# First attention's query and key projections: one 512-column matmul with the weights' high half in place of two of 256, in three banks

## The reference, cut to what matters

```python
hn = rmsnorm(h, norm_mix[l])
proj = jnp.einsum('bsd,de->bse', hn, w_in[l])
(fq, fk, fv, ff, gq, gk, gv, ga, gb, gz, gate_fox, gate_gdn) = split_in(proj)
y_fox = fox_attention(fq.reshape(...), fk.reshape(...), fv.reshape(...), log_f)
# logit[t,s] = q_t.k_s / sqrt(128) + decay, causal, softmax, times v
...
o = gated_delta_rule(q, k, v, g, beta)   # chunks of 64, a triangular solve in each
...
h = h + jnp.einsum('bse,ed->bsd', y, w_out[l])      # then a feed-forward part
```

## Time and profile before

| | |
|---|---|
| median of 3 runs | 806.86 us (806.81 to 808.23) |
| the profiled execution | 807.0 us, its span 805.6 us |
| PE busy | 798.9 us (99% of the span), granted clock 1.0 |
| DVE busy | 592.9 us (74%) |
| ACT busy | 448.9 us (56%) |
| steps 41 to 56 | from 143.34 us to about 204 us of the span |

### The profile page before, as it was taken

How to read it: one execution, slowest core, us unless ns; L and a number is a source line. 1 busy time by engine, 2 the same in 40 slices (tenths; PEclk the granted TensorE clock), 3 DMA queues, 4 the chain that set the end, 5 groups by cost and what they waited for, 6 DMA issues and landing times.

```text
span 805.6 us, 13987 instructions
## 1 busy us (share of the span) xinstructions
PE 798.9 (99%) x5608; PEld 721.3 (90%) x5608; DVE 592.9 (74%) x1001; ACT 448.9 (56%) x729; POOL 74.4 (9%) x65
## 2 busy tenths in 40 slices
PE   8999999999999999999999999999999999999998
PEld 6999998999999989899999998887878888888887
DVE  6888878875454776769999996486766777778543
ACT  6666577554535554556656564366665655655441
POOL 0001000010011203001101110021100111011000
PEclk9999999999999999999999999999999999999999
DMA  7855564547432554575687655555425656656542
GB/s 261 241 163 162 178 228 145 172 121 223 126 114 86 175 170 158 200 241 179 196 253 242 221 191 203 171 194 166 148 81 169 204 176 207 190 177 208 184 162 73
DMA packets 126257, 144.15 MB, mean 179 GB/s; under 512 B 11488, under 2 KB 103024, under 8 KB 125936
## 3 DMA queue, kind: packets, MB, share of 16 engines
q1 hardware_dynamic: 123744, 141.22, 55.1%
q10 hardware_dynamic: 2448, 2.03, 1.0%
HBM read 141.78 MB, written 1.46 MB: 178 GB/s over the span
## 4 chain that ended last, share of the span: by engine, by line
PE 97%; DMA 1%; DVE 1%; ACT 1%; SPq 0%; issue 0%; DVEq 0%; ACTq 0%
PE bank L579 94%; DMA panel_raw<-in_w_in 1%; PE bank L633 1%; PE bank L943 0%; DVE panel_lo L1557 0%; PE bank L665 0%; PE bank L892 0%; ACT panel_hi L1080 0%; PE bank L916 0%; PE bank L720 0%; ACT x_halves L1080 0%; PE bank L822 0%; SPq L2358 0%; DVE h L1986 0%; DVE h L1998 0%
## 5 line engine op out<-in xcount | busy, mean ns | idle before, releaser
L1557 DVE TENSOR_TENSOR panel_lo<-panel_raw,panel_hi 128x1024 fp32r<-128x1024 f32 x251 | 313.5, 1252 | 144.8 <-ACT panel_hi L1080 144.2
L579 PE MATMUL bank<-x_halves,panel_hi 128*128 128x256 f32 (+1 forms) x1952 | 416.0, 305 | 1.0 <-DVE x_halves L1993 0.7
L1080 ACT ACTIVATE panel_hi<-panel_raw 128x1024 fp32r<-128x1024 f32 (+1 forms) x253 | 266.8, 1057 | 164.2 <-PE bank L579 160.7
L579 PEld LDWEIGHTS bank<-x_halves,panel_hi 128*128 128x128 f32 x1952 | 315.8, 191 | 16.9 <-issue 0.9
L579 PE MATMUL bank<-x_halves,panel_lo 128*128 128x256 f32 x1152 | 324.8, 282 | 0.0
L579 PEld LDWEIGHTS bank<-x_halves,panel_lo 128*128 128x128 f32 x1152 | 219.8, 191 | 0.0
L579 PE MATMUL bank<-panel_hi,x_halves 128*128 128x512 f32 x256 | 80.6, 396 | 0.0
L579 PE MATMUL bank<-panel_hi,act_hi 128*128 128x512 f32 x176 | 68.6, 390 | 0.0
L579 PE MATMUL bank<-panel_hi,act_lo 128*128 128x512 f32 x176 | 68.5, 389 | 0.0
L579 PE MATMUL bank<-panel_lo,act_hi 128*128 128x512 f32 x176 | 68.5, 389 | 0.0
L579 PEld LDWEIGHTS bank<-panel_hi,x_halves 128*128 128x128 f32 x256 | 46.8, 188 | 9.9 <-DVE panel_lo L1557 0.6
(11 more groups left out here) (289 smaller groups left out, 927.6 us busy)
## 6 DMA issues: line engine op xcount, KB each, us to landing
panel_raw<-in_w_in SPq DMA_DIRECT2D x38, 1024.0 KB, 5.3
panel_raw<-in_w_up SPq DMA_DIRECT2D x30, 1024.0 KB, 5.4
panel_raw<-in_w_down SPq DMA_DIRECT2D x20, 1024.0 KB, 5.1
panel_raw<-in_w_gate SPq DMA_DIRECT2D x10, 1024.0 KB, 5.3
panel_raw<-in_w_out SPq DMA_DIRECT2D x8, 1024.0 KB, 5.0
panel_raw<-in_w_in SPq DMA_DIRECT2D x11, 512.0 KB, 4.6
panel_raw<-in_w_branch_fox SPq DMA_DIRECT2D x4, 1024.0 KB, 4.9
panel_raw<-in_w_branch_gdn SPq DMA_DIRECT2D x4, 1024.0 KB, 5.2
```

The lines of the kernel that those rows point to most:

```text
L579: return e.matmul(o, l, r, start=start, stop=stop, skip_group_check=True)
L1080: return e.activation(o, i_, ACT.Copy, scale=scale)
L1557: e.tensor_tensor(lo, raw_view(i, k0, kt), hi.bitcast(F32), ALU.subtract).then_inc(s_lo, 1)
```

## The change

The eight panels of fq and fk become `hl`. Each of their 16 groups takes a bank of its own from a new ring "fqk" of the banks 4, 0 and 1, in this order: fq 0: 4, 0; fk 0: 1, 4; fq 1: 0, 1; fk 1: 4, 0; fq 2: 1, 4; fk 2: 0, 1; fq 3: 4, 0; fk 3: 1, 4. The ring "side" gives up bank 4 from n = 41 and gets it back at n = 58. ACT's `fox_project` goes. In its place ACT copies the low sum of each group to SBUF (`fqk_low_copy`, 256 columns, two per panel), and DVE adds the high sum from PSUM and the copy (`fqk_sum`, 256 columns, two per panel), which empties the bank.

```diff
     for j in range(4):
         for kind, c0 in (("fq", C_FQ), ("fk", C_FK)):
-            add((kind, j), "mix", True, "w_in", 0, KD, c0 + j * PW)
+            out.append(((kind, j), "mix", "hl", "w_in", 0, KD, c0 + j * PW, PW))
...
+FQK = [(kind, j) for j in range(4) for kind in ("fq", "fk")]
...
+        fqk_low = [at(f"fqk_low{i}", [P, 2, T], 17.5, skip=2048 * i) for i in range(2)]
...
-        rings = {"few": [0, 1], "fox": [2, 3], "side": [4, 5, 6, 7], "gemm": [0, 1, 2, 3]}
+        rings = {"few": [0, 1], "fqk": [4, 0, 1], "fox": [2, 3], "side": [4, 5, 6, 7], "gemm": [0, 1, 2, 3]}
...
-            if key[0] == "z" or key in (("fv", 0), ("fq", 0), ("fk", 0)):
+            if key[0] == "z" or key == ("fv", 0):
                 return "fox"
+            if key in FQK:
+                return "fqk"
...
-        HALVES_OF = {"norm2": x_halves, "yf": yf_halves, "yg": yg_halves}
+        HALVES_OF = {"mix": x_halves, "norm2": x_halves, "yf": yf_halves, "yg": yg_halves}
...
-                e.wait_ge(*emptied(("fq", hh // 2)))
-                e.wait_ge(*emptied(("fk", hh // 2)))
+                e.wait_ge(*emptied(("fq", hh // 2, hh % 2)))
+                e.wait_ge(*emptied(("fk", hh // 2, hh % 2)))
...
+                if n == FIRST_HALF["fq", 0] + 1:
+                    rings["side"] = [5, 6, 7]
+                if n == END["fk", 3] + 2:
+                    rings["side"] = [4, 5, 6, 7]
                 gemm(n)
...
-            def fox_project(kind, j):
-                e.wait_ge(*product((kind, j)))
-                dst, scale = (qfT, float(DH) ** -0.5) if kind == "fq" else (kfT, 1.0)
-                copy(dst[:, 2 * j:2 * j + 2, :], pairs(bank_of((kind, j))), scale).then_inc(empties((kind, j)), 1)
+            def fqk_low_copy(kind, j):
+                p = FQK.index((kind, j))
+                for m in range(2):
+                    if p >= 2:
+                        e.wait_ge(*emptied((*FQK[p - 2], m)))
+                    e.wait_ge(*product_of((kind, j), m))
+                    copy(fqk_low[p % 2][:, m, :], bank_of((kind, j, m))[:, T:2 * T],
+                         float(DH) ** -0.5 if kind == "fq" else 1.0).then_inc(s_fqk_low, 1)
...
                         if n == END[kind, j]:
-                            fox_project(kind, j)
+                            fqk_low_copy(kind, j)
...
+            def fqk_sum(kind, j):
+                p = FQK.index((kind, j))
+                dst, scale = (qfT, float(DH) ** -0.5) if kind == "fq" else (kfT, 1.0)
+                for m in range(2):
+                    e.wait_ge(s_fqk_low, 2 * p + m + 1)
+                    e.scalar_tensor_tensor(dst[:, 2 * j + m, :], bank_of((kind, j, m))[:, 0:T], scale,
+                                           fqk_low[p % 2][:, m, :], ALU.mult, ALU.add).then_inc(empties((kind, j, m)), 1)
...
+                for kind, j in FQK:
+                    if n == END[kind, j]:
+                        fqk_sum(kind, j)
                 if n - 5 in FOX_AT:
                     fox_lo(FOX_AT[n - 5])
```

More of the change, by code:

```diff
@@ L442, in build @@
         s_yf_hi = sem("yf_hi")
+        s_fqk_low = sem("fqk_low_copied")
         s_gate_f, s_gate_g, s_mixed, s_y_hi, s_y = (sem(n) for n in ("gate_f_affine", "gate_g_affine", "mixed", "y_hi",
```

## The result

The changed kernel takes 809.01 us (median of 11 runs, 808.73 to 812.49); the kernel before takes 806.95 us (11 runs, 806.68 to 808.23). The ratio is 1.0029, 95% interval 1.0017 to 1.0040: slower by 2.1 us. The prediction was 808.9 us.

What follows compares the result with a forecast made beforehand. PE, busy 798.9 of 805.6 us, was taken to bound the kernel. Waits of 3.62 us less a gain of 1.60 made +2.0 us; on the median 806.86 this gave 808.9 us, range 807.5 to 811.0.

Steps and rivals of the forecast that it cites:

- DVE's unbroken stretch in 45 to 47: On DVE, 6.64 us without idle time from split to bias; the sum of fq 1 comes only after it.
- ACT's order in 51 and 53: ACT's copies of fq 2 and fk 2 move with PE; fq 2's stands behind head 1's exponentials. Waits 0.98 and 0.21 us.
- step 41, start: PE waits for bank 4 until DVE empties it of the third qk product: 0.17 us.
- middle of 43: PE waits for a sum behind DVE's small instructions of n = 42: 0.59 + 0.08 = 0.67 us.
- middle of 45: PE waits for a sum behind DVE's later split and turn: 0.35 + 0.08 = 0.43 us.
- middle of 47: PE waits for the sum of fq 1 behind DVE's unbroken stretch: 1.08 + 0.08 = 1.16 us.
- middle of 51: PE waits for ACT's copy of fq 2, then DVE's sum: 0.90 + 0.08 = 0.98 us.
- middle of 53: PE waits for ACT's later copy of fk 2, then DVE: 0.13 + 0.08 = 0.21 us.
- PE's gain: Steps 41 to 56: a pair takes 0.3475 us where a triple took 0.36; 128 pairs save 1.60 us.
- Cheaper waits: Rival: each of the six waits 0.26 us shorter, +0.5 to about +1.2; time 807.4 to 808.4, no change; chance 0.17.
- Three banks suffice: Rival: group 0's sum ends before the next step's middle, only step 41's 0.17 stays; 1.4 us less, 805.4; chance 0.05.
- The waits breed others: Rival: inversion's DRAM way or steps 49 and 55 come late too; +3.3 to +4, 810.2 to 810.9; chance 0.12.

Runs made afterwards that it cites:

- the good ring: Changed kernel with four banks ordered 6, 0, 7, 1 and DVE's sums behind fox_bias: 806.81 us; with two 256-column matmuls instead of one of 512, 807.68 us.
- the first ring: Changed kernel with four banks ordered 6, 7, 0, 1: 811.62 us; with two 256-column matmuls instead of one of 512, 811.48 us.
- the last experiment: Changed kernel, three banks, ACT's low copies first and DVE's sum of group 0 one inversion row earlier at n = 44 and 46: 807.96 us, ratio 1.0007.
- e1: Changed kernel with a fourth bank, ring 6, 7, 0, 1, small products in 4 and 5: 811.62 us, ratio 1.0059.

## Why the prediction was right, and where its sum was not

**Mechanism and place: right.** The waits stand in the middle of steps 43, 45, 47, 51 and 53, the longest at 47, none at 49 or 55, and the lag is fixed from step 57 on (3.50 to 3.43). Only 1.5 us of them, two waits, stand in the profile's view of waits, where about 3 was forecast; the rest shows in the starts alone. The copy and the sum cost what was taken for them (0.38 and 0.42 us). The two causes that the walk named, DVE's unbroken stretch in 45 to 47 and ACT's order in 51 and 53, were taken away one at a time, and each took its own stops with it.

**The sizes of the waits: 3.62 predicted, 3.09 measured.** Read from the starts given above, the excess over 0.35 plus that of the slow first pair:

| place | predicted | measured |
|---|---|---|
| step 41, start (lag 1.55 to 1.78) | 0.17 | 0.23 |
| middle of 43 | 0.67 | 0.29 + 0.10 |
| middle of 45 | 0.43 | 0.16 + 0.11 |
| middle of 47 | 1.16 | 1.00 + 0.11 |
| middle of 51 | 0.98 | 0.82 + 0.10 |
| middle of 53 | 0.21 | 0.06 + 0.11 |

In the middle of 43 the sum ends 0.34 us behind the instruction ahead of it and not 0.42, since it starts 0.08 before that one's end (152.01 + 0.16 = 152.17, and 152.09 + 0.42 = 152.51); PE starts 0.05 behind it (152.56) and not 0.09; and PE itself reaches the bank later than reckoned, since its pairs are slower. In 47 the sum costs the same 0.34 (165.04 + 0.36 = 165.40, and 165.32 + 0.42 = 165.74), and PE starts again 0.05 later. That the number holds there, 1.11 for 1.16, is luck: less the early lag of 1.55, DVE is done 0.21 us sooner than reckoned, but PE is ready 0.17 sooner too. 0.09 from DVE's end to PE, taken from one row, was too much for all of these stops; 0.08 for getting going was too little (0.10 to 0.11).

**PE's gain: 1.60 predicted, about 1.2 measured in the changed kernel, 0.95 on the good ring.** In proportion this is the term that was mis-sized most. The rate of the earlier trace rows is right where it was read: in the changed kernel's branch panels the pair still takes (294.64 - 291.86) / 8 = 0.3475:

```profile
291.86 0.28 PE L584 MATMUL bank<-yf_halves,panel_lo 128*128 128x256 f32 x1
...
294.64 0.28 PE L584 MATMUL bank<-yf_halves,panel_lo 128*128 128x256 f32 x1
```

In steps 41 to 45 it takes (151.92 - 147.32) / 13 = 0.3538, in 46 to 49 (164.44 - 161.32) / 9 = 0.3467, from 50 to 55 again 0.353; over 97 undisturbed pairs of steps 41 to 56 the mean is 0.3505, and 128 x (0.36 - 0.3505) = 1.22. I had assumed one rate for the form everywhere. It is not the stage alone that sets it: with the first four-bank ring the same steps 41 to 45 ran from 144.53 to 158.49, 13.96 us against the 14.48 of before, which is 0.013 a pair and close to what the earlier trace rows had promised.

The Trainium skill, "TensorE: Matmul & The Clock Gate", section "Wait — 56ns, not 53.3ns?", was weighed in the prediction with its 2.5 ns beyond the columns. The comparison of pairs and triples gives 0.69 us / 128 = 5.4 ns for one matmul saved on the good ring as the traces stand, 7.4 with the small stops put right, and some 9 on the first ring: neither the page's figure nor my 12.5.

**The sum.** 3.09 - 1.22 = 1.87, beside 1.95 from the lags and 2.06 from the medians. The forecast of +2.0 came out closer than its terms deserve: 0.5 us too much in the waits and 0.4 too much in the gain cancel. That is luck, and the mechanism is not.

**The rivals.** "Cheaper waits" was half right in its reason (the way to PE is 0.05) but worth 0.5 us in all, not 1.5. "Three banks suffice" fails at 47 and 51 as said; the last experiment shows that even with both queues put in order it isn't reached. "The waits breed others" didn't happen here, but did in two experiments (step 57 with four banks, step 49 with an earlier sum).

**Left open.** Why the pair takes 0.3465 in some stretches and 0.353 in others. The granted clock is 1.0 in both, and the good ring shows 0.353 in steps 46 and 47 where the changed kernel shows 0.3467. Open as well: whether a stop of 2.2 us brings the granted clock down, and whether POOL's work on `key_bias` is what slows `fox_normalise`.

## What to carry to other kernels

A bank ring's price is paid by the queue in front of its evacuation: for each reuse, ask what stands ahead of the instruction that frees the bank on its in-order engine, and check the last members of the ring against whoever takes those banks next. More banks can be slower than fewer if the order hands the wrong one to the next stage (811.6 against 807.1 us for the same four banks in another order, of which by the trace 1.5 us are a lower granted clock behind the stop). A loss that no wait explains is to be looked for in the granted clock by windows: the page's line of the clock, in 40 slices, shows 9 in each of them in that trace too. And a rate taken from one stage for the same pair of matmuls was off by a quarter to a half of the gain in another: a saving of a few ns a matmul is best measured where it is to be spent.

## What was unexpected

- The pair of 512 and 256 columns has two rates at the same granted clock, 0.3465 and 0.353 us, each steady over nine pairs and more, and which of them a step gets differs between versions of the kernel.
- A sum on DVE behind a small dependent instruction adds 0.34 us and not its 0.42, in step 43 and in step 47 alike.
- Behind the stop of 2.2 us PE worked through most of step 57 at the lower clock level, which cost 1.5 us; the profile shows no wait there.
- DVE's `fox_normalise` took 0.55 us in six traces and 0.81 and 0.89 in the two in which POOL's `key_bias` had begun before it.
- PE starts 0.05 us behind the sum that it waits for (four stops of the changed kernel; 0.09 in the earlier trace rows, about 0.15 behind the stop of 2.2 us), and its first pair then takes 0.10 to 0.11 longer.
- PE's waits for one early panel differ, with the same program up to it, from nothing to 2.3 us; one trace's span can't be set against another's before this is taken out. The trace of e1 has an early stretch at the lower clock too (0.50 from 12 to 14 us), which its net leaves out.
